# Interleaving the fifth to seventh expert's weight loads with Pool's last row store and first gathers

## The reference, cut to what matters

```
xt   = rms_norm(h)                                  # 544 rows x 1024
gi   = top1(softmax(xt @ w_group))                  # one of 4 groups
ei   = top2((xt @ w_router) within that group)      # two of its 8 experts
y    = sum over the two of  weight * (silu(xt @ w_gate[e]) * (xt @ w_up[e])) @ w_down[e]
out  = h + y
```

## Time and profile before

| what | us |
|---|---|
| median of 3 runs | 905.85 |
| lowest, highest | 904.76, 908.98 |
| the profiled execution, its device time | 905.41 |
| its span in the trace | 903.7 |
| busy: PE, DVE, ACT, Pool | 816.8, 320.2, 224.6, 166.2 |
| moved by the DMA engines | 164.65 MB, mean 182 GB/s |

### The profile page before, as it was taken

How to read it: one execution, slowest core, us unless ns; L and a number is a source line. 1 busy time by engine, 2 the same in 40 slices (tenths; PEclk the granted TensorE clock), 3 DMA queues, 4 the chain that set the end, 5 groups by cost and what they waited for, 6 DMA issues and landing times.

```text
span 903.7 us, 11379 instructions
## 1 busy us (share of the span) xinstructions
PE 816.8 (90%) x4409; PEld 499.4 (55%) x4409; DVE 320.2 (35%) x867; ACT 224.6 (25%) x467; POOL 166.2 (18%) x226
## 2 busy tenths in 40 slices
PE   5989999999999989999999999996799999787860
PEld 3465344588665765676666684554455555454430
DVE  4222655999443442122222275335300000000005
ACT  3021232112333333243334341112122222111110
POOL 3223440000332232100000001010223332222110
PEclk9999999999999999999999999998799999999995
DMA  8523020412200200303012099117899999999967
GB/s 280 157 94 119 8 94 1 145 58 87 94 1 1 94 2 0 100 1 137 4 35 59 27 411 393 63 79 274 353 413 415 414 406 378 400 389 387 385 236 296
DMA packets 54310, 164.65 MB, mean 182 GB/s; under 512 B 14596, under 2 KB 16868, under 8 KB 45520
## 3 DMA queue, kind: packets, MB, share of 16 engines
q1 hardware_dynamic: 47584, 149.86, 44.5%
q0 software_dynamic: 6672, 14.06, 4.1%
HBM read 153.65 MB, written 18.08 MB: 190 GB/s over the span
## 4 chain that ended last, share of the span: by engine, by line
PE 71%; DMA 11%; SPq 6%; DVE 3%; POOL 3%; ACT 2%; issue 2%; POOLq 0%; DVEq 0%; ACTq 0%
PE quad L803 17%; PE pair L1134 9%; PE quad L1269 6%; DMA arena<-in_w_up 6%; PE pair L997 5%; PE quad L1376 4%; PE pair L1376 4%; SPq L708 3%; PE quad L871 3%; SPq L704 2%; PE quad L1091 2%; PE pair L793 2%; PE pair L1387 2%; PE quad L1387 2%; POOL arena L1818 2%
## 5 line engine op out<-in xcount | busy, mean ns | idle before, releaser
L803 PE MATMUL quad<-ring_w,xnT 128*128 128x512 f32 (+1 forms) x192 | 79.3, 553 | 0.0
L997 PE MATMUL pair<-xnT,ring_w 128*128 128x272 f32 x256 | 70.2, 410 | 0.9 <-POOLq L1824 0.9
L1134 PE MATMUL pair<-xnT,ring_w 128*128 128x272 f32 x256 | 65.8, 403 | 0.0
L803 PE MATMUL quad<-xnT,ring_w 128*128 128x280 f32 (+1 forms) x256 | 60.6, 396 | 0.0
L1376 PE MATMUL quad<-arena,ring_w 128*64 128x256 f32 x384 | 49.3, 414 | 8.0 <-DMA arena<-in_w_up 7.3
L997 PEld LDWEIGHTS pair<-xnT,ring_w 128*128 128x128 f32 x256 | 46.4, 192 | 16.7 <-issue 7.9
L1875 POOL DMA_INDIRECT ring_w<-xn_d,idx_x x32 | 32.5, 1017 | 124.5 <-PE pair L1369 58.2
L1134 PEld LDWEIGHTS pair<-xnT,ring_w 128*128 128x128 f32 x256 | 46.5, 189 | 15.3 <-issue 6.9
L2115 DVE CUSTOM_DVE_ANT_0 arena<-quad,arena 128x528 f32<-128x528 f32 (+4 forms) x34 | 17.7, 521 | 103.9 <-PE quad L1189 60.9
L803 PEld LDWEIGHTS quad<-xnT,ring_w 128*128 128x128 f32 x256 | 48.2, 190 | 11.3 <-issue 0.8
L1376 PE MATMUL pair<-arena,ring_w 128*64 128x256 f32 x384 | 47.5, 403 | 6.0 <-DMA arena<-in_w_up 5.6
(11 more groups left out here) (271 smaller groups left out, 1233.4 us busy)
## 6 DMA issues: line engine op xcount, KB each, us to landing
arena<-in_w_gate SPq DMA_DIRECT2D x24, 1024.0 KB
arena<-in_w_up SPq DMA_DIRECT2D x24, 1024.0 KB
arena<-in_w_down SPq DMA_DIRECT2D x40, 512.0 KB
ring_w<-in_w_in SPq DMA_DIRECT2D x8, 2048.0 KB, 8.4
ring_w<-in_w_down SPq DMA_DIRECT2D x20, 512.0 KB
xnT<-in_w_gate SPq DMA_DIRECT2D x4, 1024.0 KB
xnT<-in_w_up SPq DMA_DIRECT2D x4, 1024.0 KB
hreg<-in_w_gate SPq DMA_DIRECT2D x4, 1024.0 KB
```

Of the source, the lines that this page charges most:

```text
L803: last = nc.tensor.matmul(o, l, r, start=i == 0, stop=i == len(mms) - 1)
L997: last = nc.tensor.matmul(bank[6 + job % 2][:, 0:hi - lo], chunk8(6 + cb // 4)[:, k, c0:c0 + P], xT[:, k, lo:hi], start=k == 0, stop=k == ...
L1134: last = nc.tensor.matmul(bank[6 + job % 2][:, 0:hi - lo], w[:, k, c0:c0 + P], rhs[:, k, lo:hi], start=k == 0, stop=k == kt - 1)
```

## The change

Two counters are added, `x2_sent` and `gath_sent`. Pool raises the first by one after it has issued each row store, and the second after it has issued each of the first two gathers. They count issues, not landings. SP's loop over experts 4 to 6 is written out, with waits for these counters between its transfers: gate of expert 4 at once; up and down of expert 4 when the last row store is issued; down of expert 5 when the first gather is issued; gate and up of expert 6 when the second gather is issued (before: when both had landed) and the other three conditions hold. All the transfers and their targets are the same.

```diff
+        x2_sent = sem("x2_sent")
+        gath_sent = sem("gath_sent")
...
+            def load_gate_or_up(slot, e, n, arrived):
+                sp.dma_start(moe_gu[slot][:, n * 2048:(n + 1) * 2048], (wg, wu)[n][bass.ds(e * P, P), :])\
+                    .then_inc(arrived, 16)
+
             def load_gate_up(slot, e, arrived):
-                for n, w in enumerate((wg, wu)):
-                    sp.dma_start(moe_gu[slot][:, n * 2048:(n + 1) * 2048], w[bass.ds(e * P, P), :])\
-                        .then_inc(arrived, 16)
+                for n in range(2):
+                    load_gate_or_up(slot, e, n, arrived)
...
+            def load_expert_down(n):
+                for j in range(2):
+                    load_down(n, n, j, dn_in[n])
...
             sp.wait_ge(pj_ready, pj_used[13])
-            for n in range(4, MS):
-                if n == MS - 1:
-                    sp.wait_ge(x2_ready, 2 * NT)
-                    sp.wait_ge(tr_ready, T_X2 + 2 * NT)
-                    sp.wait_ge(h_out, 16 * NT)
-                    for q in range(2):
-                        sp.wait_ge(gath[q], 16)
-                if n != 5:
-                    load_gate_up(n, n, gu_in[n])
-                for j in range(2):
-                    if n == MS - 1 and j:
-                        for i in (1, 3):
-                            sp.wait_ge(x2_stored[ORDER[i]], 16)
-                    load_down(n, n, j, dn_in[n])
+            load_gate_or_up(4, 4, 0, gu_in[4])
+            sp.wait_ge(x2_sent, NT)
+            load_gate_or_up(4, 4, 1, gu_in[4])
+            load_expert_down(4)
+            sp.wait_ge(gath_sent, 1)
+            load_expert_down(5)
+            sp.wait_ge(x2_ready, 2 * NT)
+            sp.wait_ge(tr_ready, T_X2 + 2 * NT)
+            sp.wait_ge(h_out, 16 * NT)
+            sp.wait_ge(gath_sent, 2)
+            load_gate_up(6, 6, gu_in[6])
+            for i in (1, 3):
+                sp.wait_ge(x2_stored[ORDER[i]], 16)
+            load_expert_down(6)
...
                 pool.dma_start(xn2_d[TOFF[t]:TOFF[t] + TOK[t], :], x2row[0:TOK[t], i % 2, :]).then_inc(x2_stored[t], 16)
+                nc.gpsimd.sem_inc(x2_sent, 1)
...
             for n in range(2):
                 gather(n, idx_x[:, n:n + 1], gath[n])
+                nc.gpsimd.sem_inc(gath_sent, 1)
```

## The result

The changed kernel takes 908.88 us in the median of 20 runs (906.61 to 912.3), the kernel before 905.93 us (904.76 to 909.1, 20 runs). The ratio is 1.0032, with a 95% interval of 1.0019 to 1.0044: 2.9 us slower. The span of the profiled execution is 906.8 us, 3.1 more than before. The forecast was 903.1, the range ended at 907.2.

What follows compares the result with a forecast made beforehand. DMA was taken to bound the kernel's end: the 3.1 us hole closed, less 0.3 us charged, gives 2.8 us off the profiled 905.41, so 902.6, or about 903.1 as median. Range 900.3 to 907.2 us.

Steps and rivals of the forecast that it cites:

- What bounds the kernel: Experts' stage: DMA, moving some 90 MB from 640 us without a pause, sets the end; its earlier idle time costs.
- The hole's size: DMA's idle time at 635 to 640 us: 2.7 us by share, 3.5 by rate, taken as 3.1 us to win.
- Part 1: Up and down of expert 4 wait for `x2_sent`: up 4 goes out at 624.6, no DMA gap, cost 0.
- Part 3: Down 5 waits for the first gather's issue: issued at 632.1, just meets the queue's end; 0.3 us charged.
- Part 4: Expert 6 waits for the second gather's issue: gate 6 goes 4.4 us sooner, at 633.5, and the hole is closed.
- Rival E: Counters run ahead of Pool's queued transfers, so loads get in front as before: 905.85 us, chance 0.05.
- Part 2: Last row store, with fewer loads ahead, takes 5 us; gather 0 starts at 630.9, 2.0 us sooner.
- Rival C: Last row store still takes 7.9 us beside loads; DMA dry 2.0 us from 632.7; 904.75 us, chance 0.25.
- Part 5: Expert 7's loads: gather 0 takes 4.2 us, lands at 635.1; expert 7 moves at 643.1, 1.6 us in hand.
- Rival D: Crowded gather 0 lands at 640.8, opening a second DMA hole of 2.4 us; 907.15 us, chance 0.09.
- B: Rival: fewer loads beside the store also mend DMA's rate at 621 to 636 us, 1.4 us more; 901.2, chance 0.15.
- A: The main forecast: the DMA hole before 640 us is closed, 2.8 us off; 903.1 us, chance 0.46.

Runs made afterwards that it cites:

- e10: Kernel before, with expert 6 also waiting for PE's first gate and up product; ratio 1.0063 to the kernel before, median 910.6 us.
- e1: Changed kernel with both counters raised by a tiny Pool operation behind the transfers; 904.4 us, ratio 0.9990 to the kernel before.
- e1b: The same kernel as e1, measured once more; 904.5 us, ratio 0.9976 to the kernel before.
- e8: Kernel before, with expert 6 released early by a counter raised behind the second gather's instruction; 904.2 us, ratio 0.9979 to the kernel before.
- e6: Changed kernel with only the store's counter raised by a Pool operation behind the transfer, gathers' counter plain; 906.0 us, ratio 1.0001 to the kernel before.
- e13: e7 with up 4 and all behind it also waiting for DVE's last marks; 904.2 us, ratio 0.9990 to the kernel before.
- e11: e1 with expert 4's gate sent ahead of the last h store; 907.1 us, ratio 1.0010 to the kernel before.
- e7: Changed kernel with only the gathers' counter raised behind the transfer, store's counter plain; 905.7 us, ratio 0.9995 to the kernel before.
- e12: e11 with up 4 also waiting for DVE's last marks; 903.6 us, ratio 0.9978 to the kernel before.
- e15: e1 with expert 4's gate also waiting behind the store's counter; 905.1 us in one run.

## Why the prediction was wrong, by its own steps

**What bounds the kernel: right.** The end follows the DMA engines. e10 shows it by dose (5.7 us for 2.3 MB less), and the late stage kept its rate and PE's waits for weights.

**The hole's size, 3.1 us: there, but worth less than forecast.** e1, e1b and e8, which fill it, are 0.10%, 0.24% and 0.21% under the kernel before: 0.9, 2.2 and 1.9 us, and moved 0.6 to 0.7 MB more, 1.5 to 1.7 us at 407 GB/s. The forecast for that was 2.8.

**Part 1, "up 4 goes out at 624.6", was where it failed.** I took the store's 0.61 us as over before the counter is raised. It was raised 0.6 us earlier, and up 4 went at 623.68. The same step was taken twice more, in Parts 3 and 4: down 5 went at 632.69, before gather 0 started, and gate 6 at 633.68, before gather 1 did. Rival E named this, with 0.05, but priced it at nothing; e1, which mends only this, takes the loss away, so it was the cause, and its price was 3.8 to 5.1 us (1.0032 against 0.9990 and 0.9976).

**Part 2, the store in 5 us: wrong for this kernel (8.17 us), right in direction for the change as I had read it** (3.9 to 4.1 us in e1, e1b, e6 and e13, but 7.5 in e11). Rival C had the store's 7.9 us and the dry stretch behind it, which also raised Part 3's 0.3 us to 1.3. But its reason, loads beside the store, does not hold as a rule: in e1, e1b and e6, with 0.76 us between the two, the same loads no longer slowed it. The Trainium skill (DMA: Bandwidth & Descriptors, "Queues, rings and completion order") says that the engines take turns between queues a packet at a time, and I drew from it that the depth of SP's queue is nothing to the store. The runs do not bear that out: 3.9 us in e13 and 8.2 in e7 for the same transfer, by nothing but when the loads were sent. The measurement decides.

**Part 4, "the hole is closed", and Part 5, gather 0 in 4.2 us.** It was closed, but gather 0 took 7.95 us. Rival D had that whole chain in numbers: landing at 640.8 (measured 640.84), product at 648.1 (649.04), expert 7 moving at 648.8 (sent at 649.08), with a chance of 0.09. Its sum, 1.3 us slower, was too small by two terms. The first product took 642.70 to 649.04, 6.34 us for 5.48, as the granted clock stayed at 0.50 until 648 us, 5.3 us behind the product's start; before, the rise fell 4 us behind it. The longer idle time of PE ahead of it does not account for this: in e6 gather 0 was as late, and the clock was back 3.9 us behind the start (product 5.60 us), while in e12, with an early gather, it took 6.02. What sets it stays open. And DMA ran dry at 645.6 and not 646.4. So the second hole was 4.0 us and not 2.4.

**The sum.** Hole removed, 2.7 by share; new ones at 632 to 635 us (1.3) and at 645 to 650 us (4.0): 2.6 us slower by idle share, 2.9 measured. The bytes give 12.1 - 10.6 = 1.5 MB, 3.6 us at 407 GB/s. The two lie around the measurement.

The chances were wrong in kind, too. The 0.20 for "faster" does not come out of its own terms either: half of B is 0.075 and a tenth of A is 0.046, together 0.12. I had both halves of the answer (E's cause, D's effect) as separate cases of 0.05 and 0.09, and did not see that the first makes the second likely.

## What to carry to other kernels

A plain counter step placed behind a transfer in the program does not tell that the transfer stands in a queue. Where another engine's traffic must stay behind it, let an operation on the same engine behind the transfer raise the counter, or wait for something later still (e12 and e13), and look in the timeline at which of the two issues came first. e11 shows that even then the order may not help. Where a small transfer gates a large stream (here 64 rows gate the next 2 MB of loads), price it at its crowded duration as soon as anything is sent close to it. And where DMA is the bound, count the bytes moved over the stretch, not the one hole that is visible, and compare profiles from the first point that the change can touch.

## What the runs showed of the hardware that was not expected

- Pool's plain semaphore step behind a transfer takes effect 0.01 us after the transfer's instruction starts (up 4 at 623.68 for a store from 623.67 to 624.28), and ahead of a gather's instruction of 1.13 us (counter step at 632.65, down 5 out at 632.69, gather from 632.89).
- The same 512 KB row store lands in 3.9 or 8.2 us by a difference of 0.75 us in when SP's next 1 MB transfer is issued (e1, after), and in 17 profiles nothing was seen in between: 3.3 to 4.1, or 7.5 to 8.2. The first gather goes from 3.4 to 7.95 us, with 4.8, 5.1, 5.2, 5.4, 6.1 and 6.7 in between.
- What decides between the two at a distance of 0.8 us (e11 against e1 and e15) is not settled, nor what makes a gather 3.8 us in e12 and 6.1 in e13.
